# Sixteen 1 MB weight loads of the last two experts become seven loads of 4, 2 and 1 MB

## The reference: what is computed

```python
def expert_choice_ffn(h, p):
    ...
    cap = CAPACITY_FACTOR * n // N_EXPERTS
    aff = jax.nn.softmax((xs @ p['w_router']).astype(jnp.float32), axis=-1)
    g, idx = lax.top_k(aff.T, cap)
    xe = xs[idx]
    a = jnp.einsum('ecd,edf->ecf', xe, p['w_exp_gate'])
    u = jnp.einsum('ecd,edf->ecf', xe, p['w_exp_up'])
    ye = jnp.einsum('ecf,efd->ecd', jax.nn.silu(a) * u, p['w_exp_down']) * g[..., None].astype(h.dtype)
    out = jnp.zeros((n, D), h.dtype).at[idx.reshape(-1)].add(ye.reshape(-1, D))
```

## Time and profile before

| | us |
|---|---|
| median of 3 runs | 2267.77 |
| lowest and highest | 2267.26, 2268.74 |
| the profiled execution, its own time | 2267.16 |
| its span, first to last instruction | 2265.4 |
| PE busy in the span | 2169.5 (96%) |
| DVE busy | 1073.8 (47%) |
| ACT busy | 377.3 (17%) |

### The profile page before, as it was taken

How to read it: one execution, slowest core, us unless ns; L and a number is a source line. 1 busy time by engine, 2 the same in 40 slices (tenths; PEclk the granted TensorE clock), 3 DMA queues, 4 the chain that set the end, 5 groups by cost and what they waited for, 6 DMA issues and landing times.

```text
span 2265.4 us, 26459 instructions
## 1 busy us (share of the span) xinstructions
PE 2169.5 (96%) x10773; PEld 1375.5 (61%) x10773; DVE 1073.8 (47%) x1704; ACT 377.3 (17%) x953; POOL 139.5 (6%) x144
## 2 busy tenths in 40 slices
PE   6999999999999999999999999999988988889997
PEld 3499964467899999999987753333332322223233
DVE  5198998776778678676663430111011010102114
ACT  3011110012444432000001221011110000000002
POOL 0011100013111110000000000100000000000000
PEclk9999999999999999999999999999999999999998
DMA  9964553342442434545464389999999999999997
GB/s 399 426 232 186 213 200 145 153 180 94 186 164 102 182 142 156 191 162 198 160 257 154 124 311 418 420 428 428 427 432 430 430 432 431 429 432 430 431 425 299
DMA packets 47101, 647.83 MB, mean 286 GB/s; under 512 B 5350, under 2 KB 5896, under 8 KB 9352
## 3 DMA queue, kind: packets, MB, share of 16 engines
q1 hardware_dynamic: 44792, 637.66, 68.6%
q10 hardware_dynamic: 2192, 8.52, 0.9%
HBM read 642.47 MB, written 3.69 MB: 285 GB/s over the span
## 4 chain that ended last, share of the span: by engine, by line
PE 75%; DMA 18%; DVE 3%; DVEq 2%; issue 1%; ACT 1%; ACTq 0%; POOL 0%; SPq 0%; POOLq 0%
PE PS L1015 27%; DMA ring<-in_w_gate_up_late 15%; PE PS L1730 12%; PE PS L869 5%; PE PS L1773 5%; PE PS L1498 4%; PE PS L1192 3%; PE PS L1482 2%; PE PS L858 2%; PE PS L1179 2%; PE PS L1665 2%; PE PS L1806 1%; PE PS L1841 1%; DMA ring<-in_w_gate_up 1%; PE PS L1646 1%
## 5 line engine op out<-in xcount | busy, mean ns | idle before, releaser
L2628 DVE SCALAR_TENSOR_TENSOR GXE<-ring,SM,GXE 128x512 f32<-128x512 f32 x450 | 329.7, 771 | 17.4 <-issue 1.3
L1730 PE MATMUL PS<-ring,RF 128*48 128x512 f32 x1200 | 280.7, 608 | 35.3 <-DMA ring<-in_w_gate_up_late 32.2
L1015 PE MATMUL PS<-RB,ring 128*128 128x192 f32 x1376 | 233.3, 327 | 0.8 <-ACT GXE L1982 0.8
L1015 PEld LDWEIGHTS PS<-RB,ring 128*128 128x128 f32 x1376 | 224.9, 190 | 6.9 <-ACT GXE L1982 2.0
L3523 DVE TENSOR_TENSOR RB<-RB,PS 128x512 f32<-128x512 f32 x84 | 55.7, 684 | 349.8 <-PE PS L1665 349.7
L1730 PEld LDWEIGHTS PS<-ring,RF 128*48 128x48 f32 x1200 | 81.0, 125 | 221.6 <-issue 183.9
L3528 DVE TENSOR_TENSOR GXE<-RF,PS 48x512 f32<-48x512 f32 x32 | 22.1, 690 | 291.1 <-ACT RF L2283 262.4
L1015 PE MATMUL PS<-GXE,ring 128*128 128x192 f32 x768 | 130.1, 326 | 0.0
L869 PE MATMUL PS<-ring,RB 128*128 128x512 f32 x288 | 126.9, 593 | 0.0
L1015 PEld LDWEIGHTS PS<-GXE,ring 128*128 128x128 f32 x768 | 124.9, 190 | 0.1
L1730 PE MATMUL PS<-GXE,RF 128*48 128x512 f32 x448 | 110.2, 610 | 10.7 <-DMA GXE<-in_w_gate_up_late 10.6
(11 more groups left out here) (454 smaller groups left out, 2979.6 us busy)
## 6 DMA issues: line engine op xcount, KB each, us to landing
ring<-in_w_gate_up_late SPq DMA_DIRECT2D x28, 4096.0 KB, 21.5
ring<-in_w_ada SPq DMA_DIRECT2D x48, 2048.0 KB, 9.9
ring<-in_w_in SPq DMA_DIRECT2D x38, 2048.0 KB, 8.9
GXE<-in_w_gate_up_late SPq DMA_DIRECT2D x10, 4096.0 KB, 21.8
ring<-in_w_gate_up SPq DMA_DIRECT2D x19, 2048.0 KB, 15.0
ring<-in_w_down_late SPq DMA_DIRECT2D x8, 4096.0 KB, 21.8
GXE<-in_w_down_late SPq DMA_DIRECT2D x8, 4096.0 KB, 21.7
ring<-in_w_gate_up SPq DMA_DIRECT2D x26, 1024.0 KB, 12.0
```

The costliest lines, as they stand in the source:

```text
L1015: last = mm(bank(b, TH), w(k), x(k), start=start and k == 0, stop=k == kn - 1, skip_group_check=not start)
L1730: last = mm(bank(n, p0=64 * u, p1=64 * u + SLOTS), xeT[:, 0, kk, :] if first else x_cur[:, kk, :], weights_at(e, 2 * i + u, k * FF + n * NC_),
L2628: last = stt(out=acc[c], in0=w, scalar=cond[:, kk, c:c + 1], in1=acc[c], op0=ALU.mult, op1=ALU.add)
```

## The change

The sixteen loads of one quarter become seven. Quarters 0 to 3 are one load of 4 MB, 4 to 7 another; 8 and 9, 10 and 11, 12 and 13 are one load of 2 MB each; 14 and 15 stay single loads of 1 MB. The host lays the weights out so that what one load brings lies in one row for each partition: 32 KB, 16 KB or 8 KB. The homes are the same, and so is what PE computes and in which order. PE now waits only ahead of the first quarter of a load (`q == joined_with(q)`), and then for the whole load. SP issues a joined load under the wait of its quarters; the load of 12 and 13 waits for what 13 waited for.

```diff
         def quarter_landed(q):
-            n = QUARTER_SEM[quarter_slot(q)]
+            n = QUARTER_SEM[quarter_slot(joined_with(q))]
...
-            return quads_on + (16 if n in UNIT_SEM else 0) + 16 * (q // 12 + 1)
+            return quads_on + (16 if n in UNIT_SEM else 0) + (32 if 12 <= q < 15 else 16)
...
+        def joined_with(q):
+            return q // 4 * 4 if q < 8 else q // 2 * 2 if q < 14 else q
...
-                for q in range(16):
-                    if q < 4:
-                        sp.wait_ge(piece_used, base + 14 + 8)
-                    elif q < 8:
-                        sp.wait_ge(piece_used, base + 14 + 12)
-                    elif q < 10:
-                        sp.wait_ge(piece_used, base + 28)
-                    elif q < 12:
-                        sp.wait_ge(gu_done, 2 * e + 4)
-                    elif q % 2 == 0:
-                        sp.wait_ge(piece_used, base + 28 + (quarter_slot(q) // 2 + 1))
-                    else:
-                        sp.wait_ge(down_done, 2 * e + (quarter_slot(q) // 2 + 1))
-                    sp.dma_start(down_homes[quarter_slot(q)], down_quarter(q % 4 // 2, q // 4, q % 2))\
-                        .then_inc(quarter_in[quarter_slot(q)], 16)
+                sp.wait_ge(piece_used, base + 14 + 8)
+                sp.dma_start(quads[2], w_down_quads[0]).then_inc(quarter_in[0], 16)
+                sp.wait_ge(piece_used, base + 14 + 12)
+                sp.dma_start(quads[0], w_down_quads[1]).then_inc(quarter_in[4], 16)
+                sp.wait_ge(piece_used, base + 28)
+                sp.dma_start(quads[1][:, 0:4 * FF], w_down_units[0]).then_inc(quarter_in[8], 16)
+                sp.wait_ge(gu_done, 2 * e + 4)
+                sp.dma_start(quads[1][:, 4 * FF:8 * FF], w_down_units[1]).then_inc(quarter_in[10], 16)
+                sp.wait_ge(down_done, 2 * e + 1)
+                sp.dma_start(quads[2][:, 0:4 * FF], w_down_units[2]).then_inc(quarter_in[0], 16)
+                sp.wait_ge(piece_used, base + 28 + 3)
+                sp.dma_start(down_homes[4], w_down_last[0]).then_inc(quarter_in[4], 16)
+                sp.wait_ge(down_done, 2 * e + 3)
+                sp.dma_start(down_homes[5], w_down_last[1]).then_inc(quarter_in[5], 16)
...
                 def down_part(c, d, r):
                     q = 4 * c + 2 * d + r
-                    pe.wait_ge(quarter_in[quarter_slot(q)], quarter_landed(q))
+                    if q == joined_with(q):
+                        pe.wait_ge(quarter_in[quarter_slot(q)], quarter_landed(q))
```

More of the change, by code:

```diff
@@ L77, in build @@
 def build(nc, x_prompt, x_sample, cache_k, cache_v, cols, w_ada, w_in_first, w_in, qk_g, w_attn_o, f1_w, f_vec, f2_w,
-          f3_w, w_hy_o, w_out, w_router, w_gate_up, w_down, w_gate_up_late, w_down_late, w_down_last, tabs, dft, zfeat, decay, rope,
+          f3_w, w_hy_o, w_out, w_router, w_gate_up, w_down, w_gate_up_late, w_down_late, w_down_quads, w_down_units, w_down_last, tabs, dft, zfeat, decay, rope,
           y_prompt, y_sample, state_k, state_v):
@@ L632, in down_rows @@
                 return w_down[ds(e * (HYH * P) + i * P, P), :]
-            def down_quarter(d, c, r):
-                return w_down_last[d, c, r]
             def piece_free(e, q):
@@ L3681, in quarter_tiles @@
     w = w.reshape(2, 2, 2, P, 2, 4, NC_)
-    return np.ascontiguousarray(w.transpose(0, 5, 1, 3, 2, 4, 6)).reshape(2, 4, 2, P, 4 * NC_)
+    q = w.transpose(5, 3, 0, 1, 2, 4, 6).reshape(4, P, 2, 2, 4 * NC_)
+    quads = q[0:2].reshape(2, P, 16 * NC_)
+    units = np.stack([q[2, :, 0], q[2, :, 1], q[3, :, 0]]).reshape(3, P, 8 * NC_)
+    return quads, units, np.stack([q[3, :, 1, 0], q[3, :, 1, 1]])
 def unit_pairs(w):
@@ L3749 @@
         ("w_gate_up", gate_up[:6].reshape(6 * HK * P, 4 * FF)), ("w_down", down[:6].reshape(6 * HYH * P, 2 * D)),
-        ("w_gate_up_late", unit_pairs(gate_up[6:])), ("w_down_late", unit_pairs(down[6:NE - 2])), ("w_down_last", quarter_tiles(a["w_exp_down"][0][NE - 2:])),
+        ("w_gate_up_late", unit_pairs(gate_up[6:])), ("w_down_late", unit_pairs(down[6:NE - 2])),
+        *zip(("w_down_quads", "w_down_units", "w_down_last"), quarter_tiles(a["w_exp_down"][0][NE - 2:])),
         ("tabs", tabs), ("dft", dft), ("zfeat", zfeat), ("decay", decay), ("rope", rope),
```

## The result

The changed kernel is slower: 2277.03 us median (2275.52 to 2277.52, 6 runs) against 2268.26 us (2266.91 to 2269.16, 6 runs) for the kernel before, 8.8 us. The ratio is 1.0037, with an interval of 1.0027 to 1.0048, that is 6 to 11 us. Timed a second time beside other kernels it took 2275.42 us against 2268.58 us, a ratio of 1.0032 (1.0020 to 1.0044).

The account below looks back on a forecast made before the run. PE was taken to bound the down stage, with loads just hidden; a 5.5 us stop plus 2.1 us of low clock made 7.6 us, forecasting 2275.4 us, range 2272.8 to 2278.4.

Parts of the forecast that it names:

- likeliest case: Whole kernel: slower through PE's stop and low clock, 2272.8 to 2278.4 us, given a chance of 0.83.
- the sum: Down stage: stop 5.5 us plus clock 2.1 us make 7.6 us (6.6 to 8.3), so 2275.4 us.
- The signs: Changed profile: DMA left at about 2215.5, first 4 MB landing 20.5 us after issue, quarter 4 starting at about 2226.
- signs of being wrong: Wait under 3 us, the part behind it shorter by as much, or the stretch ahead of 2196 moved.
- What bounds the stage: Down stage: PE sets the end; the sixteen weight loads are hidden, but only just.
- The stop ahead of quarter 0: After gate and up, PE waits for the first 4 MB load: 5.5 us (5.5 to 5.7).
- The clock: After the stop PE's granted clock falls, costing 2.1 us, with 1.5 and 2.6 as ends.
- The floor at quarter 4: The second 4 MB load, landing at 2225.2, makes the shift at least 6.6 us, whatever the clock does.
- The 2 MB loads, SP's later waits, the rest: Quarters 8 to 15 land 6 us or more ahead; SP issues before the queue runs dry; no cost.
- Covered: Rival: the stop ahead of quarter 0 is hidden, time stays 2267.8 us; chance 0.09.
- The pace of the whole stream: Rival: new arrays speed all loads, mean 435 GB/s against 428, giving 2263.3 us; chance 0.03.
- The last loads come late: Rival: loads 14 and 15, issued later, make PE wait another 5.8 us, 2281 us; chance 0.05.

Follow-up runs that it names:

- e8: The changed kernel profiled and timed again without an edit, against the kernel before: 2275.42 us, ratio 1.0032.
- e1: Changed kernel with its three new weight arrays, but sixteen single loads and sixteen waits, nothing joined: 2267.40 us, ratio 0.9996 against the kernel before.
- e6: Kernel before with its sixteen 1 MB loads from the old array, but PE waiting in groups as in the change: 2277.06 us, ratio 1.0035 against the kernel before.
- e3: Changed kernel with quarters 4 to 7 as four single loads again, the rest joined: 2275.34 us, ratio 1.0029 against the kernel before.
- e7: Changed kernel plus ten unread products on PE ahead of quarter 0's wait: 2274.85 us, ratio 1.0029 against the kernel before.
- e2: Changed kernel with quarters 0 to 3 as four single loads again, the rest joined: 2277.75 us, ratio 1.0036 against the kernel before.
- e4: Changed kernel with quarters 0 to 7 as eight single loads, only the 2 MB pairs joined: 2271.34 us, ratio 1.0012 against the kernel before.

## Why the prediction was right

The time, 2277.03 us, lies in the range, and in the likeliest case at that; the second timing, 2275.42, is on the number. The mechanism held: PE stops ahead of quarter 0 for the last byte of the first 4 MB, runs on at a low clock, and nothing behind it gives the time back. The sizes in the first profile fit in part by luck: there the stage cost 6.1 us, under the 7.6 of the sum and even under its floor of 6.6, and the 3.8 us that the execution lost ahead of the stage made up for it. In e8 the stage cost 7.5 us, and 0.7 lay ahead.

*The signs.* In the first profile the chain left the DMA engines at 2218.24 and not at about 2215.5, the load landed 18.8 us after its issue and not 20.5, and quarter 4 started at 2228.57 and not at about 2226; in e8 these are 2216.17, 20.9 and 2226.80. Of the signs of being wrong one came: the stretch ahead of 2196 has moved, by 3.8 us and in e8 by 0.7. The prediction took it as fixed. That the change didn't move it rests on e8 and on e1, which has the new arrays and no lateness.

*What bounds the stage.* That PE sets the end and the loads are only hidden holds: e1 changes the transfers' rows and arrays and e6 leaves them all alone, and the time follows the waits in both.

*The stop ahead of quarter 0.* Forecast at 5.5 us, 5.5 to 5.7. It measured 4.60, 5.66, 5.68 and 5.92 in the four profiles that have it whole (the change, e8, e3, e6); in e7, with the added products in it, it is 5.58 from the end of gate and up to quarter 0. The short one is the first profile of the change: the stop's end is set by the loads and its start by PE, and there the load landed 2.7 us later than forecast and gate and up ended 3.8 us later. So the term is right where the two keep the distance that they had in the profile of before, and off by 1 us where they don't. I had taken this distance as fixed.

*The wait is for the whole load.* PE starts 0.14 us after the landing in the chain, in the change and in e6. The Trainium skill, page "DMA: Bandwidth & Descriptors", section "Why a DMA increments its semaphore by 16 and not by 1", says that only the full 16 means that all data has landed, and that a value on the way there does not tell which bytes have. The traces agree as far as they go: in these chains PE starts behind the landing, and no run let it in on a lower value. e6 shows the same from the other side, since a wait for four separate loads gives the stop of one large one.

*The clock.* Taken as 2.1 us from rows at 1.5 and 2.6. Against the 3.45 us that quarters 0 and 1 take in the chain of before it measured 4.98 - 3.45 = 1.5 in the first profile, 1.8 in e8, 2.4 in e3 and 2.7 in e6; with the stop, each adds up to what its stage lost. The ends were about right, and the value is an execution's own. The step itself, that the clock falls because the stop is longer than two others behind which it fell, was weaker than it looks: rows 6 show two stops with a loss, and the same profile has a stop of 2.74 us without one (last section). e7 shows that the loss hangs on PE's standing still: with the products in the stop the clock stayed up.

*The floor at quarter 4.* It hangs on the same distance as the stop, so the first profile's stage, at 6.1 us, could come out under it. It did not decide the change's own time, as forecast for a clock loss over 1 us: the second 4 MB had landed 0.5 us ahead of quarter 4. And where the clock loss was taken away it came out, 6.65 us against 6.6 (e7). e2 shows that the second join would cost as much alone.

*The 2 MB loads, SP's later waits, the rest.* None was waited for, and their cover is the stop, as e4 shows. From quarter 4 to the last scatter the chain has the same rows, 30.19 us against 30.20.

*The rivals.* "Covered" falls with the first wait row. "The pace of the whole stream" falls with e1. One reading under it holds only for slices of 56.6 us: no slice lies above 435 GB/s, but the stretches of a few us in the earlier trace rows read 439 and 452. "The last loads come late" did not happen: no wait for them in any profile.

*The sum.* 7.6 us against 8.8 and, timed again, 6.8, with intervals from 4.5 to 11. Both agree with it, and I can't say more: the 3 us by which the two profiles of the changed kernel differ ahead of the stage are larger than the gap. What makes the loads of one execution land later there, and the 0.3 us behind the last scatter, stay open.

## What to carry to other kernels

Before joining loads, ask when the first byte is wanted and how far behind the last one lands: where the consumer keeps pace with the stream, a load of n pieces in place of one can make it start up to n - 1 pieces later. Here that was three pieces of 2.47 us less the 1.7 us by which quarter 0 was ahead, and the larger rows gave back only some 0.2 us for each 4 MB. Such a delay was paid once, by the load that is latest against its need, not once for each join; so undoing one of the two large joins gained nothing. And where the small loads already move at nearly the pace of the large ones, as 424 against 432 GB/s here, there is little for larger loads to win.

## What the runs showed of the hardware

The same stop gave PE a different loss from execution to execution: after the 4.15 to 4.17 us of idle at about 1680, the 32 matmuls that take 7.10 us at full clock took 9.74 in the profile of before, 8.77 and 9.54 in the two of the change, and 8.41 in e3.

For shorter stops the length does not tell whether the clock falls. In the changed kernel a stop of 2.27 us ahead of the stage was followed by a low clock (timeline of PE, then the stretch behind the stop, where it reads 0.53):

```profile
2169.65 8.77 PE L1805 MATMUL PS<-ring,RF 128*48 128x512 f32 x32 [2.27 <-DMA ring<-in_w_gate_up_late]
...
2169.65:2173.30 3.65, 3.65 (x10) 1.04 (x12) 0.00 (x0) 0.00 (x0) 0.00 (x0) 0.53 1.00 431
```

In e3 a stop of the same length at the same place was not:

```profile
2167.06 7.07 PE L1813 MATMUL PS<-ring,RF 128*48 128x512 f32 x32 [2.27 <-DMA ring<-in_w_gate_up_late]
```

And the profile of before has, beside the one of the earlier trace rows, two more stops of 2.74 us; behind the first the matmuls were slow, behind the second they were not:

```profile
1785.09 8.77 PE L1730 MATMUL PS<-ring,RF 128*48 128x512 f32 x32 [2.74 <-DMA ring<-in_w_gate_up_late]
...
2019.72 7.07 PE L1730 MATMUL PS<-ring,RF 128*48 128x512 f32 x32 [2.74 <-DMA ring<-in_w_gate_up_late]
```

What decides between the two, no run shows.
